# Three pairs of Strassen products in place of six directly multiplied output tiles, the memory keys' statistics two heads at a time, and x brought back in two transfers

## The reference

```python
def _sq_relu_mlp(h, w1, w2):                       # w1 1024x4096, w2 4096x1024
    return jnp.square(jax.nn.relu(h @ w1)) @ w2
...
        y_x = _sq_relu_mlp(_modulate(x, g_pre_mlp[l], sh2, sc2), w_mlp_in[l], w_mlp_out[l])
        x = x + gt2 * _rmsnorm(y_x, g_post_mlp[l])
...
def second_block(x, mem, ...):
        h = rmsnorm(x, norm_mix[l])
        mem_h = rmsnorm(mem, norm_mem[l])
        proj = h @ w_in[l]
...
def mem_group(q_raw, mem_h, w_mem_kv, q_norm, k_norm):
    kv = (mem_h @ w_mem_kv).reshape(B, M, 2, MEM_HEADS, MEM_HEAD_DIM)   # 4 heads of 128, 256 memory rows
    k = rmsnorm(kv[:, :, 0], k_norm)
```

## Time and profile before

| | |
|---|---|
| median of 3 runs | 1293.27 us (1292.88 to 1294.02) |
| profiled execution, its own time | 1292.5 us |
| profiled execution, span from first to last instruction | 1291.2 us |
| PE busy | 1279.5 us of the span |
| POOL busy | 823.0 us of the span |

### The profile page before, as it was taken

How to read it: one execution, slowest core, us unless ns; L and a number is a source line. 1 busy time by engine, 2 the same in 40 slices (tenths; PEclk the granted TensorE clock), 3 DMA queues, 4 the chain that set the end, 5 groups by cost and what they waited for, 6 DMA issues and landing times.

```text
span 1291.2 us, 22880 instructions
## 1 busy us (share of the span) xinstructions
PE 1279.5 (99%) x8718; PEld 1136.3 (88%) x8718; DVE 963.8 (75%) x1685; ACT 781.5 (61%) x1488; POOL 823.0 (64%) x592
## 2 busy tenths in 40 slices
PE   9999999999999999999999999999999999999998
PEld 6787778879999999988788788777789999999998
DVE  5796694878778989834468575747589887987888
ACT  4532585479677585865655557645577655765664
POOL 3643434979778687656467372644378876877785
PEclk9999999999999999999999999999999999999999
DMA  9685235353333333523332112120223223333233
GB/s 379 239 314 215 84 135 207 110 184 107 115 108 99 112 101 99 180 98 106 123 113 81 44 59 72 60 66 33 66 82 115 99 99 104 106 102 115 99 104 110
DMA packets 42125, 156.35 MB, mean 121 GB/s; under 512 B 4384, under 2 KB 5152, under 8 KB 40992
## 3 DMA queue, kind: packets, MB, share of 16 engines
q1 hardware_dynamic: 41136, 151.60, 33.9%
q0 software_dynamic: 448, 2.62, 0.5%
q10 hardware_dynamic: 432, 0.67, 0.1%
HBM read 149.90 MB, written 4.19 MB: 119 GB/s over the span
## 4 chain that ended last, share of the span: by engine, by line
PE 80%; DVE 9%; ACT 4%; POOL 4%; issue 2%; DMA 1%; DVEq 0%; SPq 0%; ACTq 0%; POOLq 0%
PE bank L879 22%; PE bank L881 22%; PE bank L880 21%; PE bank L1437 2%; POOL wL L3804 2%; PE bank L928 1%; PE bank L930 1%; PE bank L929 1%; PE bank L982 1%; POOL acc L3814 1%; DVE small L2942 1%; PE bank L975 1%; PE bank L942 1%; PE bank L1674 1%; PE bank L967 1%
## 5 line engine op out<-in xcount | busy, mean ns | idle before, releaser
L3804 POOL TENSOR_TENSOR wL<-raw,wH 128x1024 fp32r<-128x1024 f32 (+1 forms) x91 | 227.3, 2503 | 225.5 <-ACT wH L1815 222.4
L879 PE MATMUL bank<-hH,wH 128*128 128x512 f32 (+1 forms) x544 | 211.0, 388 | 1.6 <-POOL wL L3804 0.6
L881 PE MATMUL bank<-hH,wL 128*128 128x512 f32 (+1 forms) x544 | 200.6, 369 | 0.0
L880 PE MATMUL bank<-hL,wH 128*128 128x512 f32 (+1 forms) x544 | 200.4, 368 | 0.0
L3809 POOL TENSOR_TENSOR wL<-raw,wH 128x512 fp32r<-128x512 f32 (+1 forms) x120 | 154.2, 1286 | 31.2 <-ACT wH L1824 30.6
L879 PE MATMUL bank<-gH,wH 128*128 128x256 f32 x512 | 145.4, 284 | 0.3 <-POOL gL L3809 0.3
L880 PE MATMUL bank<-gL,wH 128*128 128x256 f32 x512 | 144.9, 283 | 0.0
L881 PE MATMUL bank<-gH,wL 128*128 128x256 f32 x512 | 144.9, 283 | 0.0
L1815 ACT ACTIVATE wH<-raw 128x1024 fp32r<-128x1024 f32 (+1 forms) x91 | 95.2, 1048 | 54.6 <-PE bank L881 28.2
L879 PEld LDWEIGHTS bank<-hH,wH 128*128 128x128 f32 x544 | 102.9, 189 | 25.0 <-issue 6.5
L881 PEld LDWEIGHTS bank<-hH,wL 128*128 128x128 f32 x544 | 102.6, 189 | 17.9
(11 more groups left out here) (537 smaller groups left out, 4083.7 us busy)
## 6 DMA issues: line engine op xcount, KB each, us to landing
raw<-in_wall SPq DMA_DIRECT2D x211, 512.0 KB, 3.3
rows<-in_wall SPq DMA_DIRECT2D x24, 1024.0 KB, 11.2
bra<-in_rpbw SPq DMA_DIRECT2D x8, 360.0 KB, 4.7
...
xT<-in_xn SPq DMA_DIRECT2D x1, 2048.0 KB, 8.4
out_x<-xT SPq DMA_DIRECT2D x1, 2048.0 KB, 8.6
xT<-out_x SPq DMA_DIRECT2D x1, 2048.0 KB, 9.1
...
```

What stands on the lines that cost most here:

```text
L879: matmul(o, a_h, b_h, start=first, stop=False)
L880: matmul(o, a_h, b_l, start=False, stop=False)
L881: return matmul(o, a_l, b_h, start=False, stop=last)
L3804: tt(wL[i % NHL][:, 0:n], raw[load(c) % NRAW][:, 0:n], wH[i % NHL][:, 0:n].bitcast(F32), ALU.subtract).then_inc(s.w_lo, 1)
```

## The change

The last quarter gets three outer pairs for the output tiles 0 to 5 (`outer` 12, 13 and 14, so G grows by three); tiles 6 and 7 stay direct, in halves as before, and read the forms of the quarter, with one more piece of their own, the late tokens of the even tiles (`xlast`), which ACT and POOL split into `xlH` and `xlL` during pair 13. The square sums of y (`result_square`, `result_sum`, buffers `ysum` and `ysq`) and the keys' squares (`memory_squares`, `ksq`, `ksqH`, `ksqL`, two heads at a time) are moved between and behind the last two pairs, the statistics of the keys stand in PE's queue behind products 4 and 6 of the last pair, and DVE scales the keys after it has added tiles 6 and 7's first halves. x comes back by two transfers behind the last pair.

The core of the diff:

```diff
-OUT_ORDER = [24 + i for i in (0, 1, 2, 3, 4, 5, 7, 6)]
+OUT_ORDER = range(24, 32)
+
+Y_ORDER = (1, 0, 3, 2, 5, 4)
...
-             + [("outer", 4 * quarter + j) for j in range(4 if quarter < 3 else 0)]]
+             + [("outer", 4 * quarter + j) for j in range(4 if quarter < 3 else 3)]]
...
+    ksq = at("ksq", R + 64 * K, [128, 1024])
+    xlast = at("xl", 88 * K, [128, 4, 256])
+    xlH = at("xlH", R + 56 * K, [128, 4, 256], F32R)
+    ysum = at("ysum", R + 72 * K, [128, 512])
+    ysq = [at("ysq", R + (74 + 2 * i) * K, [128, 512]) for i in range(2)]
...
+        KEY_PLACE = {(G - 1, 4): 0, (G - 1, 6): 1}
+        def memory_statistic(i):
+            statistic_of_halves(f"mk{i}", 512, BANK["mk", i])
...
+                if (n, q) in KEY_PLACE:
+                    memory_statistic(KEY_PLACE[n, q])
...
-        for m in range(6):
-            b = BANK["w_mlp_out", m]
-            if m >= 2:
-                tile("w_mlp_out", m, OUT_ORDER, [(claim(b), XB)])
-            freed[b] = s.y_full, m + 1
-            if 0 < m < 5:
-                statistic_of_halves(f"mk{m - 1}", 256)
...
+        def late_high():
+            act.wait_ge(s.relu_sq, 2 * 15)
+            act.wait_ge(s.prod, 7 * (INNER[13] + 1))
+            copy(xlH[:, :, :], xlast[:, :, :], s.full)
+        def memory_squares():
+            act.wait_ge(s.k_mem, 4)
+            activation(ksq[:, :], kvM[:, 0:2, :].rearrange("p a t -> p (a t)"), ACT.Square).then_inc(s.head_sq, 4)
+            act.wait_ge(s.head_sq, 4)
+            activation(ksqH[:, :], ksq[:, :], ACT.Copy).then_inc(s.sums_hi, 2)
+        def result_square(i):
+            act.wait_ge(s.y, Y.half + 24 + i + 1)
+            if i > 2:
+                act.wait_ge(s.add_g, ADD_G.f + i - 2)
+            square((ysq[i % 2] if i else ysum)[:, :], y[:, Y_ORDER[i], :], s.sq)
...
             piece_high(n + 1, 2)
+            if outer_of(n) == 13:
+                late_high()
             piece_high(n + 1, 3)
...
+            if outer_of(n) == 13:
+                result_square(0)
+                result_square(1)
+                memory_squares()
...
+                first_product(n)
+                ahead("w_mlp_out", OUT_ORDER[0], 6, 2)
+                result_square(2)
+                result_square(3)
+                memory_root(0)
...
         act.wait_ge(s.lb_v, 3)
         activation(lb[:, 1, :], lb[:, 1, :], ACT.Exp).then_inc(s.lb_a, 1)
         activation(lb[:, 2, :], lb[:, 2, :], ACT.Exp).then_inc(s.lb_a, 1)
+        ahead("w_mlp_out", OUT_ORDER[0], 6)
+        result_square(4)
+        result_square(5)
+        memory_root(1)
...
+        def memory_key(i):
+            dve.wait_ge(s.root, rooted(f"mk{i}"))
+            dve.wait_ge(s.ones, 5)
+            stt(out=kvM[:, i, :], in0=kvM[:, i, :], scalar=vc("mem_k"), in1=kroot[:, 512 * i:512 * i + 512],
+                op0=ALU.mult, op1=ALU.mult).then_inc(s.mk_n, 2)
...
         last_tiles(0)
+        memory_key(0)
+        memory_key(1)
...
+        def result_sum(i):
+            pool.wait_ge(s.sq, SQ.f + i + 1)
+            if i > 1:
+                pool.wait_ge(s.add_g, ADD_G.f + i - 1)
+            tt(ysum[:, :], ysum[:, :], ysq[i % 2][:, :], ALU.add).then_inc(s.add_g, 1)
...
             if n + 1 == G:
-                ahead("w_mlp_out", 24, 0, 2)
+                result_sum(1)
+                pool.wait_ge(s.sums_hi, halved("mk1") + 1)
+                tt(ksqL[:, :], ksq[:, :], ksqH[:, :].bitcast(F32), ALU.subtract).then_inc(s.sums_lo, 2)
+                ahead("w_mlp_out", OUT_ORDER[0], 6, 2)
+                result_sum(2)
+                result_sum(3)
                 continue
...
             piece_rest(n + 1, 3)
+            if outer_of(n) == 13:
+                pool.wait_ge(s.full, FULL.b + 33)
+                rest(xlL[:, :, :], xlast[:, :, :], xlH[:, :, :], s.rest_g)
...
+        ahead("w_mlp_out", OUT_ORDER[0], 6)
+        result_sum(4)
+        result_sum(5)
...
-            if i == last_inner:
-                sp.wait_ge(s.prod, outer_done(2))
+            if i == first_f + 2:
+                sp.wait_ge(s.prod, 7 * G)
                 sp.wait_ge(s.x_moved, 32)
-                nc.sync.dma_start(xT[:, :, :], out).then_inc(s.x_moved, 16)
+                nc.sync.dma_start(xT[:, 0:4, :], out[:, 0:4, :]).then_inc(s.x_moved, 16)
+                nc.sync.dma_start(xT[:, 4:8, :], out[:, 4:8, :]).then_inc(s.x_rest_in, 16)
```

More of the change, by code:

```diff
@@ L433 @@
 SQ = before(x=8, c=8, xt=8, f=10, h3=8, lat=5, om=4, x2=12)
-ADD_V = before(x=4, c=7, m=7, xt=1, s2=16, b=48, h3=1, half=16, x2=1, fs=44)
+ADD_V = before(x=4, c=7, m=7, xt=1, s2=16, b=64, h3=1, half=16, x2=1, fs=44)
 ADD_G = before(y=7, f=7, lat=3, om=3, x2=3)
 SILU = before(c=2, q=4, gg=4, g=22)
-Y = before(mix=8, half=24)
+Y = before(mix=8, half=30)
 Y_SQ = before(m=8, y=8)
@@ L441 @@
 MULT = before(hc=8, h2=8, b=3)
-FULL = before(first=16, hm=8, h2=4, b=24, fs=22)
+FULL = before(first=16, hm=8, h2=4, b=33, fs=22)
 REST = before(first=8, hm=4, h2=8, fs=22)
-REST_G = before(first=8, hm=4, s2=4, b=24, form=4, fb=22)
+REST_G = before(first=8, hm=4, s2=4, b=33, form=4, fb=22)
 X2_S = before(x2=8, up=22)
@@ L458, in normed @@
     return NORMS.index((which, j - j % 2))
-ROOTS = ("x ctx mem mix pre_mlp mk0 mk1 mk2 mk3 post_a post_b h3 mq hg0 hg1 hg2 hg3 lq lk q k "
+ROOTS = ("x ctx mem mix pre_mlp mk0 mk1 post_a post_b h3 mq hg0 hg1 hg2 hg3 lq lk q k "
          "om ol ffn").split()
@@ L469, in rooted @@
     return 2 * ROOTS.index(name) + 2
-HALVED = "mk0 mk1 mk2 mk3 lq".split()
+HALVED = "mk0 mk1 lq".split()
 def halved(name):
@@ L1354, in half_statistic @@
             pe.wait_ge(s.sq, SQ.f + 8 + 2 * i)
-            matmul(o, ones[:, :], acc[0][:, 256 * i:256 * i + 256], start=True, stop=False)
+            matmul(o, ones[:, :], ysum[:, 256 * i:256 * i + 256], start=True, stop=False)
             matmul(o, ones[:, :], tm[3][:, 256 * i:256 * i + 256], start=False, stop=True).then_inc(s.summed, 1)
@@ L3277, in vector_program @@
         tt(coef[:, 4, :], mod[:, 40:48, 0], vcs("g_post_mlp"), ALU.mult).then_inc(s.coef_c, 1)
-        low_sums("mk0")
-        for m in range(6):
-            dve.wait_ge(s.product, out_done(max(m, 1)))
-            dve.wait_ge(s.y, Y.half + 24)
-            tt(y[:, m, :], y[:, m, :], bank[BANK["w_mlp_out", m]], ALU.add).then_inc(s.y_full, 1)
-            if 0 < m < 4:
-                low_sums(f"mk{m}")
-            if 0 < m < 5:
-                dve.wait_ge(s.root, rooted(f"mk{m - 1}"))
-                dve.wait_ge(s.ones, 5)
-                stt(out=kM[:, m - 1, :], in0=kM[:, m - 1, :], scalar=vc("mem_k"), in1=rs[(m - 1) % 2][:, 0:256],
-                    op0=ALU.mult, op1=ALU.mult).then_inc(s.mk_n, 1)
         def last_tiles(i):
@@ L3957, in gpsimd_program @@
             piece_rest(n + 1, 6)
-        for m in range(8):
-            if m not in (1, 7):
-                ahead("w_mlp_out", OUT_ORDER[4 if m == 0 else 0], m)
-            if 0 < m < 6:
-                if m > 1:
-                    pool.wait_ge(s.add_g, ADD_G.f + m - 1)
-                add_squares(acc[0][:, :], m, s.sq, SQ.f)
+        ahead("w_mlp_out", OUT_ORDER[0], 6)
+        result_sum(4)
+        result_sum(5)
         def late_squares(i):
@@ L3969, in late_squares @@
             pool.wait_ge(s.add_g, ADD_G.f + 5)
-            tt(acc[0][:, t], acc[0][:, t], tm[2][:, t], ALU.add).then_inc(s.add_g, 1)
+            tt(ysum[:, t], ysum[:, t], tm[2][:, t], ALU.add).then_inc(s.add_g, 1)
         late_squares(0)
```

168 lines of the change are left out of this document (59 added, 109 removed).

## The result

The changed kernel took 1296.18 us (median of 15 runs, 1294.60 to 1296.76), the kernel before on the same chips 1293.16 us (1292.36 to 1294.02). The ratio is 1.0019, with a 95% interval of 1.0012 to 1.0026, so the change made the kernel slower. The medians lie 3.0 us apart, the means 2.5 (1295.73 and 1293.20). The forecast was 1296.3.

A forecast was written before the change was run, and what follows sets the result against it. PE bounds the kernel, but POOL's longer queue makes the half statistic 1.37 us later, plus 0.9 and 0.8 of DVE port costs: 3.07. 1292.5 + 3.07 = 1295.6, median 0.77 above: 1296.3 us, range 1294.2 to 1299.2.

The forecast's parts named there:

- PE's saving: On PE, three new pairs with key statistics replace six direct tiles: 31.63 us instead of 33.71, saving 2.08.
- POOL's queue: POOL from piece 3 of the last pair to `late_squares(0)`, 578.82 to 601.6, making PE 1.37 us later than before.
- The first wait: PE idles some 1.8 us ahead of `mk0` in the last pair for POOL's `ksqL`, adding nothing to the end.
- The forecast wait of 3.4: PE idles about 3.4 us ahead of `half_statistic(0)`, until POOL's `ysum` ends it.
- 0.9 for the keys' scaling: Two DVE `stt` of 512 columns beside POOL's last sums cost POOL 0.9 us more.
- 0.8 for the small instructions: DVE's `lb` instructions held amid POOL's chunks delay ACT's last chunk by 0 to 1.64 us; half, 0.8, was taken.
- The 0.44 for each `stt`: POOL time lost per 512-column DVE `stt` beside it, from a POOL piece taking 1.74 us instead of 1.30.
- The 1.44 by full exclusion: POOL's loss to the two key-scaling `stt` if DVE and POOL exclude each other fully: 0.72 us each, median near 1297.0.
- the row at 223.06: Earlier trace row: a DVE instruction of 8 columns took 0.91 us until POOL's chunk ended; the next took 0.15.
- Tiles 6 and 7 up to `half_statistic(0)` keep their 600.29 - 592.74 = 7.55: PE's stretch behind the last pair stays 7.55 us, so without any wait the statistic would be reached at 598.21.
- The clock: a rival at 0.10: Clock falls to 1.2 GHz behind PE's new waits, slowing 33 matmuls after the statistic: up to 1299.9 us, chance 0.10.
- the likeliest case: Statistic 3.07 us later through POOL's queue and DVE port costs, median 1296.3 us, own range 1294.7 to 1297.3, chance 0.72.

The follow-up runs named there:

- again: The changed kernel run once more without any edit, timed against the kernel before: 1295.63 us, ratio 1.0022.
- The last variant: Changed kernel with POOL's third weight chunk, first keys' statistic, keys' scaling, DVE's small instructions and ACT's exponentials placed later, `ksqL` made on DVE: 1291.22 us, ratio 0.9986.
- keys_late: Changed kernel with DVE's scaling of the keys moved behind both halves of the second norm, a single run: 1294.59 us.
- chunk_late: Changed kernel with POOL's third weight chunk moved behind the last sums of squares: 1293.36 us, ratio 1.0002 to the kernel before.
- lb_early: Changed kernel with DVE's small gate instructions and ACT's two exponentials moved ahead of the last pair's sums: 1295.61 us, ratio 1.0018 to the kernel before.
- mk_later: Changed kernel with the first keys' statistic moved from behind product 4 of the last pair to behind product 5: 1296.08 us, ratio 1.0023.

## Why the prediction was right, and where not

**Direction and place: right.** PE's saving is eaten by a wait for POOL's sums of squares ahead of `half_statistic(0)`, and the chunk that stands ahead of the last two sums is what makes POOL late: moved back, it brings the ratio from 1.0022 (`again`) to 1.0002 on the same chip.

**PE's saving.** Forecast 2.08 us, 31.63 for the pairs and statistics. Measured 592.97 - 559.39 = 33.58, less the 1.64 by which `mk0` was late (from 587.46, where the matmul behind 587.34 was due, to 589.09): 31.94, a saving of 1.77. The first pair took 10.69 instead of 10.38, for it waits for POOL's `pL`. The last variant, almost without waits, is 1.78 ahead of the kernel before at the statistic: this is what the scheme is worth here.

**POOL's queue.** Piece 3 started 19.78 behind the first outer pair, forecast 19.79. Without what DVE cost it (0.19 gap, 0.26 on the last sum) the queue took 23.15, forecast 22.77; four dependent sums cost more than was counted. The first wait was 1.64 by the starts (1.48 idle), forecast 1.8. The forecast wait of 3.4 ended by `ysum` did not show as such: PE stood 1.97 for DVE's y and then 0.3 for POOL's last sum.

**DVE beside POOL: mis-sized, and its path missed.** The step put 0.9 for the keys' scaling and 0.8 for the small instructions, 1.7 in all. It was 0.26 (keys_late) and the gap of 0.19, 0.45. This takes 1.25 from the forecast 3.07 and the longer queue adds 0.38, in all 2.20; the statistic came 2.22 later in an execution at full clock. The 0.44 for each `stt` was not wrong in kind (chunk_late's 0.25 and 0.44); but DVE reached them at 600.88, not 598.8, when little of POOL's queue ahead of the statistic was left. The 1.44 by full exclusion, as the other forecast had it, was further off. The small instructions were held as the row at 223.06 had it, 0.82 to 2.35 each, but their harm went another way: not through ACT's chunk, but through the additions queued behind them on DVE, to the bank of tile 6. "Tiles 6 and 7 up to `half_statistic(0)` keep their 600.29 - 592.74 = 7.55" was the step that failed there: it took 602.87 - 592.97 = 9.90. It cost nothing of its own: PE would have stood at the statistic at 602.58, and POOL's sum ended at 602.77. But it had to go too before anything could be gained.

**The clock: a rival at 0.10 that happens in about half of the executions.** (The prediction's "no PE wait over 0.8 us" passes over the next row of its view, 1.3 us ahead of the kernel's first matmul.) Runs with a mean clock under 1.000: with PE idle for 1.81 ahead of the bank 7 of 15 and 6 of 11, for 2.23 ahead of the statistic 6 of 11 (lb_early), for 3.20 nine of 11 (mk_later); in the six variants whose longest idle stretch here was 1.65 us or less none of 66. The single run of keys_late, with 1.80 ahead of the bank, had none either. Its price was overrated: 3.6 us for all 33 matmuls behind the statistic, against 1.5 between the groups. In the profile that shows it the fall began ahead of the statistic, slowed 15 matmuls by 0.09 each, of which 1.1 us reached the statistic, and was over soon behind it. The Trainium skill (TensorE: Matmul & The Clock Gate, section "HAM oscillation — how this bites in real kernels") describes such a throttling of bursts behind idle time. These runs agree in kind, with 0.54 and 0.50 in the stretches above, and add that the same kernel does it in one execution and not in the next.

So the median of 1296.18 against 1296.3 owes much to luck: the likeliest case as written, a steady clock and 1.7 us of port costs, did not happen. The terms that held give 1.8 to 2.2 us, and the runs at full clock have a median of 1294.92, 1.4 under the forecast. The clock adds 1.5 in the executions in which it falls; they are nearly half, and this carries the median up to the forecast. Two misses of about the same size, the port costs set too high and the clock held to be steady, cancelled.
